# Two-layer mixer and expert kernel: weights in half blocks, expert row rings of five and six, and a reordered context prologue

## The reference, cut to what matters

```
mod = silu(c) @ ada_w[l] + ada_b[l]                  # 6 vectors of 1024: shift, scale, gate for mixer and experts
h = rmsnorm(x, norm_mix_g) * (1 + sc_m) + sh_m
proj = h @ w_in                                      # 1024 x 2048: q, k, v, hyena (3 x 256), gmlp (2 x 256)
mixed = concat(attention(q, k, v), hyena(...), chunk_gmlp(...)) @ w_out
x = x + g_m * mixed
h = rmsnorm(x, norm_ffn_g) * (1 + sc_f) + sh_f
s = (h @ peer_wq) . peer_keys                        # 8 heads x 2 halves x 128 keys
idx, gate = the best 16 of 16 x 16 pairs of keys, softmax over their scores     # per token and head
a = gelu(h . peer_u[idx]);  x = x + g_f * sum(gate * a * peer_v[idx])           # 128 experts per token
```

## Time and profile before

| | |
|---|---|
| median of 3 runs | 4637.51 us (4630.89 to 4637.74) |
| profiled execution, its own time | 4663.97 us |
| its span | 4662.2 us |
| TensorE / VectorE / ScalarE / GpSimd busy | 74% / 56% / 24% / 60% |
| moved by DMA | 1503.70 MB, mean 323 GB/s |
| mean granted TensorE clock | 0.876 |

### The profile page before, as it was taken

One profiled execution on the slowest core, in us unless ns is written; L12 is line 12 of the kernel. 1 busy time (PEld: TensorE's weight loads), 2 busy tenths in 40 slices (PEclk: granted clock), 3 DMA queues, 4 the chain that ended last, 5 costly groups with the idle time before them and its releaser, 6 DMA issues.

```text
span 4662.2 us, 37811 instructions
## 1 busy us (share of the span) xinstructions
PE 3442.7 (74%) x11256; PEld 1602.1 (34%) x11256; DVE 2632.0 (56%) x6503; ACT 1122.8 (24%) x2533; POOL 2806.0 (60%) x2564
## 2 busy tenths in 40 slices
PE   7869868766577767777776898786766676677777
PEld 3733434323123334332222444442322222222223
DVE  2166656456455565556666565564665666666661
ACT  3423223121212222212121432231211212121212
POOL 0035555566555666667777344565667777777774
PEclk8889888888788888889889899888878999998899
DMA  7468898789999999899999687887899999999997
GB/s 295 143 234 301 311 338 296 278 301 336 346 367 341 358 341 336 332 359 363 348 352 360 216 286 297 318 307 282 327 334 352 356 365 354 357 362 347 367 358 279
DMA packets 394680, 1503.70 MB, mean 323 GB/s; under 512 B 44396, under 2 KB 46126, under 8 KB 376432
## 3 DMA queue, kind: packets, MB, share of 16 engines
q0 software_dynamic: 368640, 1342.34, 78.9%
q1 hardware_dynamic: 25840, 158.96, 8.8%
HBM read 1498.24 MB, written 2.88 MB: 322 GB/s over the span
## 4 chain that ended last, share of the span: by engine, by line
POOL 30%; PE 24%; issue 18%; DMA 17%; DVE 7%; ACT 3%; SPq 0%; another core or an unknown queue 0%; DVEq 0%; POOLq 0%; ACTq 0%
POOL rows_ring L605 16%; POOL rows_ring L616 14%; DMA rows_ring<-in_peer_v,idx 7%; DMA rows_ring<-in_peer_v,turned_idx 7%; PE psum L928 6%; PE psum L920 5%; DVE rows_ring L1465 3%; PE psum L854 3%; PE psum L706 3%; DMA rows_ring<-in_peer_u,idx 2%; DMA ring<-in_ada 1%; PE psum L651 1%; PE psum L693 1%; PE psum L839 1%; PE psum L886 1%
## 5 line engine op out<-in xcount | busy, mean ns | idle before, releaser
L605 POOL DMA_INDIRECT rows_ring<-in_peer_u,idx x1280 | 1453.1, 1135 | 1198.5 <-DVE rows_ring L1465 587.3
L928 PE MATMUL psum<-rows_ring,diag 128*128 128x512 f32 x3072 | 1591.3, 667 | 634.0 <-DMA rows_ring<-in_peer_v,idx 581.4
L1465 DVE SCALAR_TENSOR_TENSOR rows_ring<-rows_ring,area 128x1024 f32<-128x1024 f32 x1280 | 1549.5, 1223 | 718.9 <-DMA rows_ring<-in_peer_u,idx 679.7
L928 PEld LDWEIGHTS psum<-rows_ring,diag 128*128 128x128 f32 x3072 | 618.4, 212 | 1567.2 <-issue 1453.3
L616 POOL DMA_INDIRECT rows_ring<-in_peer_v,idx x768 | 812.1, 1057 | 297.8 <-issue 211.3
L920 PE MATMUL psum<-rows_ring,diag 128*64 128x512 f32 x2048 | 641.1, 757 | 385.4 <-DMA rows_ring<-in_peer_v,turned_idx 376.8
L616 POOL DMA_INDIRECT rows_ring<-in_peer_v,turned_idx x512 | 540.5, 1056 | 334.2 <-PE psum L920 180.3
L1165 ACT ACTIVATE diag<-ident,turn 128x128 f32<-128x128 f32 x768 | 303.3, 401 | 1663.0 <-PE psum L928 1189.1
L920 PEld LDWEIGHTS psum<-rows_ring,diag 128*64 128x64 f32 x2048 | 160.4, 161 | 712.5 <-issue 661.5
L706 PE MATMUL psum<-area,ring 128*128 128x128 f32 (+1 forms) x832 | 240.9, 446 | 6.5 <-DMA ring<-in_win 6.5
L1474 DVE SCALAR_TENSOR_TENSOR turn<-acts,gate_s,gate_e 128x16 f32<-128x16 f32 x80 | 18.8, 235 | 382.3 <-ACT acts L1135 233.6
(11 more groups left out here) (185 smaller groups left out, 2864.3 us busy)
## 6 DMA issues: line engine op xcount, KB each, us to landing
ring<-in_ada SPq DMA_DIRECT2D x48, 1024.0 KB
ring<-in_win SPq DMA_DIRECT2D x32, 1024.0 KB
ring<-in_wout SPq DMA_DIRECT2D x24, 1024.0 KB
ring<-in_wq SPq DMA_DIRECT2D x24, 1024.0 KB
rows_ring<-in_peer_u,idx POOLq DMA_INDIRECT x1280
ring<-in_dft SPq DMA_DIRECT2D x12, 1024.0 KB
rows_ring<-in_peer_v,idx POOLq DMA_INDIRECT x768
rows_ring<-in_peer_v,turned_idx POOLq DMA_INDIRECT x512
```

The costliest lines, as they stand in the source:

```text
L605: pool.indirect_dma_start(row(0, k), None, peer_u, bass.IndirectOffsetOnAxis(ap=idx[v % IDX_PLACES][:, k:k + 1], axis=0)).then_inc(row_lan ...
L928: m = pe.matmul(acc[:, b, :], diag[:, (r + j) % 4, :], row(1, r + j)[:, b * 512:(b + 1) * 512], start=first and j == 0, stop=last and j == 1)
L1465: dve.scalar_tensor_tensor(out=row(0, k), in0=row(0, k), scalar=1.0, in1=h, op0=ALU.mult, op1=ALU.mult, accum_out=dots[:, k:k + 1]).then_i ...
```

## The change

`SLOTS` becomes 5, `HALF` is 1024 columns: weights come in half blocks (0.524 MB) into five places, 20 KB a partition instead of 32. `ROWS` becomes (5, 6): five rows for peer_u, six for peer_v. In `step_jobs` the `down` runs five places ahead and the `up` six (`spread` stays at four). `STREAM` is no longer written out: `blocks_of` names the half blocks that a job reads, and they are loaded in the order of first use in ORDER and freed after the last. The first 40 half blocks of layer 0's modulation go round the 11 places of the row rings, which no expert uses yet. SyncE still issues all loads in one order.

The context pass of layer 0 starts its mixer behind modulation block 3; blocks 4 to 9 stand among its jobs, 10 and 11 behind the first pick and the first gathers in the list (`_late`). The latent norm and filter of layer 0 move to the latent mixer, as in layer 1. `xT` is loaded in two parts: the context columns with four constants after eight half blocks, the latent ones with the rotary table and `swap` ahead of the first `wq` block (`latent_loads`). `dots` is doubled, so that `dot` waits for the gelu of two units before. VectorE walks `DVE_ORDER`, which gets the same jobs as `ORDER`; a function `behind` is added and not called.

```
-SLOTS = 4
-ROWS = 4
+HALF = BLOCK // 2
+SLOTS = 5
+ROWS = (5, 6)
@@ input_jobs
     if st == C_ and l == 0:
-        jobs = js("mod:0 mod:1 modT:0 mod:2 modT:1 mod:3 modT:2 mod:4 modT:3 rms:0 mod:5 modT:4 f1:0 mod:6 modT:5 f2:0 ")
-        jobs += latent("rms:0") + js("mod:7 modT:6 f3:4 mod:8 modT:7 hf:4") + latent("f1:0") + js("mod:9 modT:8")
-        jobs += latent("f2:0") + js("mod:10 modT:9 mod:11") + latent("f3:0 f3:1 f3:2 f3:3") + js("modT:10 modT:11")
...
+        jobs = js("mod:0 mod:1 modT:0 mod:2 modT:1 mod:3 modT:2 f1:0 modT:3 rms:0 f2:0 mod:4 f3:4 qk:0 modT:4 vt:4 hf:4 hs:0 "
+                  "hy:0 mod:5 ko:0 hy:1 modT:5 hy:2 hy:3 mod:6 hy:4 hy:5 modT:6 su:0 ut:0 su:1 mod:7 qk:1 sp:0 hs:1 modT:7 "
+                  "qk:2 hs:2 qk:3 mod:8 sp:1 hs:3 qk:4 modT:8 df:4 hs:4 mod:9 cv:0 cv:1 modT:9")
...
-        jobs = js("rms:0 f1:0 f2:0 f3:0 f3:1 f3:2 f3:3 hf:0 hf:1 hf:2 hf:3") if l else []
+        jobs = js("rms:0 f1:0 f2:0 f3:0 f3:1 f3:2 f3:3 hf:0 hf:1 hf:2 hf:3")
@@ step_jobs
-        unit("down", v + (k + ROWS) // TOPK, (k + ROWS) % TOPK)
+        unit("down", v + (k + ROWS[0]) // TOPK, (k + ROWS[0]) % TOPK)
-            pair("up", r + ROWS)
-            pair("spread", r + ROWS)
+            pair("up", r + ROWS[1])
+            pair("spread", r + 4)
@@
+_late = [("mod", 0, C_, 10), ("mod", 0, C_, 11), ("modT", 0, C_, 10), ("modT", 0, C_, 11)]
-ORDER, _taken = input_jobs(0, C_) + output_jobs(0, C_, 0) + _first, 0
+ORDER, _taken = input_jobs(0, C_) + output_jobs(0, C_, 0) + _first + _late, 0
+DVE_ORDER = list(ORDER)
@@
+def blocks_of(job):
+    kind, l, st, n = job
+    some = {"mod": ("ada", range(4 * n, 4 * n + 4)), "qk": ("win", [11 + n if n else 0]), "vt": ("win", range(1, 4)),
+            "hy": ("win", [4 + n]), "su": ("win", [10 + n]), "wo": ("wout", [n]), "wq": ("wq", [n])}
+    if st == L_:
+        some.update({"hf": ("dft", range(4)), "df": ("dftu", range(4)), "cv": ("dftu", range(4, 8))})
+    if kind in ("ka", "kb"):
+        some[kind] = ("keys", [1 if n > 1 else 0])
+    name, places = some.get(kind, ("", []))
+    return [(name, l, st, i) for i in places]
+
+LAST_USE = {}
+for _job in ORDER:
+    for _block in blocks_of(_job):
+        LAST_USE[_block] = (_job[0] + "_mm", done(*_job))
+STREAM = list(LAST_USE.items())
...
+    if _block[:2] == ("ada", 0) and _block[3] < 40:
+        _p, _n_rows = SLOTS + _n_rows % sum(ROWS), _n_rows + 1
+    else:
+        _p, _n_ring = _n_ring % SLOTS, _n_ring + 1
@@ SyncE
-                if n == SLOTS:
+                if n == 8:
                     small_loads(0)
                     const_loads()
-                if n >= SLOTS:
-                    name, value = STREAM[n - SLOTS][1]
+                if (kind, l, st, i) == ("wq", 0, C_, 0):
+                    latent_loads()
+                if FREED[n]:
+                    name, value = FREED[n]
                     sp.wait_ge(s[name], value)
@@ VectorE
-                if v and k == 0:
-                    dve.wait_ge(s["gelu_ready"], v)
+                if v > 1 and k == 0:
+                    dve.wait_ge(s["gelu_ready"], v - 1)
```

More of the change, by code:

```diff
@@ L210, in weave @@
 def weave(mixer, experts):
-    total, cost, taken, out = sum(ROOM[j[0]] for j in mixer), 0, 0, []
+    total, cost, taken, out = sum(ROOM[j[0]] for j in mixer) or 1, 0, 0, []
     for job in mixer:
@@ L219, in weave, with behind, stretch @@
     return out + experts[taken:]
-_first = [("pick", 0, 0, p) for p in range(PICK_PARTS)] + [("gexp", 0, 0, 0)] + [("down", 0, 0, k) for k in range(ROWS)]
+_first = [("pick", 0, 0, p) for p in range(PICK_PARTS)] + [("gexp", 0, 0, 0)] + [("down", 0, 0, k) for k in range(ROWS[0])]
 _steps = [_job for _v in range(len(UNIT) + 2) for _job in step_jobs(_v)]
-ORDER, _taken = input_jobs(0, C_) + output_jobs(0, C_, 0) + _first, 0
[L227 to L231, removed]
+_late = [("mod", 0, C_, 10), ("mod", 0, C_, 11), ("modT", 0, C_, 10), ("modT", 0, C_, 11)]
+ORDER, _taken = input_jobs(0, C_) + output_jobs(0, C_, 0) + _first + _late, 0
+DVE_ORDER = list(ORDER)
+def behind(jobs, n):
+    out, held, dots = [], [], 0
+    for job in jobs:
+        if job[0] in ("dot", "pick", "down", "up"):
+            while held and held[0][0] <= dots:
+                out.append(held.pop(0)[1])
+            dots += job[0] == "dot"
+            out.append(job)
+        else:
+            held.append((dots + n, job))
+    return out + [job for _, job in held]
+def stretch(mixer, upto, also=0):
+    global ORDER, DVE_ORDER, _taken
+    end = _steps.index(upto) + also
+    jobs = weave(mixer, _steps[_taken:end])
+    ORDER += jobs
+    DVE_ORDER += jobs
     _taken = end
@@ L280 @@
 TURNED_BEFORE = {j: TURNED[i - 1] for i, j in enumerate(TURNED) if i}
[L283 to L307, removed]
-            for _i in range(2, 4):
-                _b("dftu", _i, "cv_mm", "cv", 1)
-        for _part, (_t, _end) in enumerate(PARTS[_st]):
-            for _i in range(4 * _part, 4 * _part + 4):
-                _b("wout", _i, "wo_mm", "wo", 2 * _i + 1)
-            for _i in range(4 * _part, 4 * _part + 4):
-                _b("wq", _i, "wq_mm", "wq", 2 * _i + 1)
-            _b("keys", _part, "kb_mm", "kb", 2 * _end - 1)
@@ L486, in mixer_peer_kernel @@
         y_stored = [sem("y_stored0"), sem("y_stored1")]
-        landed = [sem(f"landed{k}") for k in range(SLOTS)]
-        row_landed = [[sem(f"{name}_landed{k}") for k in range(ROWS)] for name in ("down", "up")]
+        landed = [sem(f"landed{k}") for k in range(PLACES)]
+        row_landed = [[sem(f"{name}_landed{k}") for k in range(n)] for name, n in zip(("down", "up"), ROWS)]
         def qk_dst(st, n):
@@ L1505, in _ @@
             dve.tensor_tensor(stacked[:], ident[:, 0:64], ident[:, 64:128], ALU.add).then_inc(s["stacked_ready"], 1)
-            for job in ORDER:
+            for job in DVE_ORDER:
                 kind, a, b, n = job
```

158 lines of the change are left out of this document (88 added, 70 removed).

## The result

The changed kernel takes 4278.47 us (median of 4 runs, 4274.45 to 4289.31) against 4637.62 us for the kernel before, a ratio of 0.922 with a 95% interval of 0.9181 to 0.9259. I had forecast 4557 us. The direction was right and the size was not: 359 us less instead of 80.

A forecast was written before the change was run, and what follows sets the result against it. It took the expert-row gathers, holding 78.9% of the DMA engines' span, as the bound. Its terms, -62 + 35 - 70 + 12 + 5 = -80 us, took 4637.5 to 4557 us; range 4465 to 4635, the sum's own 4515 to 4600.

The forecast's parts named there:

- Part 1: Prologue: reordered loads and context mixer bring the first gather to 189 us, 62 us earlier, bounds 45 to 75.
- Part 2: First stage behind the first gather: moved latent and modulation work costs 35 us, between 5 and 48.
- Part 3: Row rings of 5 and 6: 70 us gained, about 10 in expert stretches; bounds nothing to half of 421.
- the cap of 421 us: All stages behind the prologue: the DMA's idle time, (1 - share) x length, limits what longer row rings can gain.
- the average wait of 2.9 us: GpSimd at the first ring: 587.3 / 200, the period of one row, so one row more can swallow a typical wait.
- Part 4: Weights in half blocks, five places: costs 12 us, between 0 and 210, plus 5 us for smaller packets.
- Part 5: VectorE's order list, unused `behind` and doubled dots: no instruction moves, 0 us.
- B: Row rings buy a third of the idle DMA, 140 us: 4487 us; chance 0.17.
- A: Row rings buy nothing, as TensorE and the DMA set the woven stages: 4617 us; chance 0.19.
- C: Slower: half blocks of weights come late behind the first gather, up to 4753 us at 1 us lateness; chance 0.14.
- Rival D: Moved latent work costs all it saved, 48 with only 45 won at the front: 4587 us; chance 0.50.
- the signs that I had named: Row-ring waits clearly below 850 us, woven stages' DMA share up 0.03 or so, expert stretches' rates hardly moving.

The follow-up runs named there:

- e11: Kernel after with the latent norm and filter of layer 0 back in the context pass, in one piece behind its convolution: 4284.88 us, ratio 0.9213.
- e1: Kernel after with both row rings back at four rows, the rest of the change kept: 4662.39 us, ratio 1.0018 to the kernel before.
- e6: Kernel after with row rings of four and four and eight half-block places for the weights instead of five: 4633.52 us, ratio 0.9949.
- e7: Kernel after with second-table gathers of 512 columns instead of 1024, a quarter less DMA traffic, sums wrong: 4329.90 us, ratio 0.9307.
- e15: Kernel after with VectorE's dots in two halves and second-table gathers of 512 columns, sums wrong: 4121.72 us, ratio 0.8849.
- e3: Kernel after with four rows for the first table and six for the second: 4376.48 us, ratio 0.9399.
- e2: Kernel after with five rows for the first table and four for the second: 4653.91 us, ratio 1.0004.
- e10: Kernel after with rings of four and four and the second table's gathers two places ahead of the add instead of four: 5504.72 us, ratio 1.1821.
- e13: Kernel after with five rows for each table: 4603.31 us, ratio 0.987.
- e16: Kernel after with each VectorE dot in four pieces of 256 columns: 4215.87 us, ratio 0.9051.

## Why the prediction was wrong, by its own steps

**Part 1 was right in its time, by errors that cancel.** The first gather came at 191.7 us for 189. The key projection began at 55.84, 8 us later than I had it: the norm's first square came at 41.30 for 34 and the norm took 11.4 us for 10.2, while the second sine and the filter product cost no more than I had. The chain from there to the end of the convolution took 62 us for 65, and the latent tokens cost nothing at the first query block. e11 shows what the 59 us hang on: with the latent norm and filter back in front, in one piece, nothing of them remains. So they are mostly work moved behind the first gather. What the new order would bring with these jobs spread among others, as they stood before, was not tried.

**Part 2 was about right, with a reservation.** The stage became 470 us for 475 forecast. With the old rings, however, units 0 to 8 take 530 us for 470 (e1), 519 with eight weight places (e6), so the moved work costs 49 to 60 us there and I had 35; the longer rings gave 36 back. With the old rings and eight weight places the whole reordered prologue brings 0.5% (e6), 24 us for my 27.

**Part 3 is the step that failed: 384 us for 70** (e1 against the kernel after; 371 by the ratios). That is also beyond the 210 us that I had named as the upper bound. Three readings in it were wrong.

First, the cap of 421 us from (1 - DMA share) x length. The share counts time in which packets are under way, not what could be moved: the same share of 0.97 to 1.01 held 357, 387 and 399 GB/s, and a quarter fewer bytes changed no expert unit (e7, e15). So I held the expert stretches for full and gave them 10 us; they gave 94 + 35 = 129 us. By their own sum they were GpSimd's: 32 x (1.11 + 0.30) = 45.1 us and about 1.8 us of waits make the 47.0 of before, and 32 x (1.053 + 0.30) = 43.3 make the 43.6 of after. So about half of what a unit gained is waits and half is shorter issues. Why they became shorter stays open. Between the 57th and the 80th list 104 issues took over 1.3 us, for 151 before; but e3, where GpSimd hardly waits for a dot there (0.7 us in 1100), has 179, an issue mean of 1.125 us and therefore a unit of 45.8.

Second, the rings' waits taken by name. 587 us against 263 made the first ring look like the one to lengthen, and its one new row the one that counts. It is worth nothing alone (e2). Much of the wait for VectorE came from the second table's ring, passed on through one common order of jobs: it fell by 204 us in e3 and rose by 975 in e10 with the first ring unchanged. Whether the late row itself (theory B of e10) or the gathers held up behind it (theory D of e10) weighs more is not shown.

Third, the average wait of 2.9 us set against one row's period. An add takes two rows, so one pair is the step in which the second ring works (e13). I tried to get the size from the round trip of a pair. The issues of the kernel after from 3144 to 4210, with the median us to landing behind the comma:

```profile
rows_ring<-in_peer_u,idx POOLq DMA_INDIRECT x391, 6.4
rows_ring<-in_peer_v,idx POOLq DMA_INDIRECT x364, 6.4
```

A pair costs two issues of 1.35 us, that landing, an add of some 2 us, and up to two gathers of the first table queued ahead: some 14 us, an estimate from these rows. Set against the average time that two pairs bridge it does not explain the gain. In the expert stretch before they bridge 2 x 47 / 8 = 11.8 us, less than 14, and yet GpSimd waited there only 23 of 1160 us for the second ring. In units 8 to 16 they bridge 2 x 479 / 64 = 15 us, more than 14, and there the two rows brought 59 us. What is shown is where they help, beside mixer jobs (239 of 268 us in e3). That a mixer job ahead of an add uses up a margin so small, and the third pair covers it, is argued and not shown.

**Part 4 was under-sized:** the five places cost 29 us (e6 against e1) for 12. The 5 us for smaller packets were not tried by themselves; the hardware queue moved its 158.97 MB in 10.1% of 4272 us, 368 GB/s for 387 before, near the 365 that I had as the worst. **Part 5** was not tried by itself.

**Rivals.** B had the sign and named the second table's side, and 140 us of 384. A would have left as they were; C was the right fear for 29 us. Rival D, which I gave the largest chance, holds with the old rings: e1's first list comes 60 us earlier and its units 0 to 8 take 60 us longer. It says nothing of the rings, and they made the result. None had the second ring's pairs as what counts, and my range of 4465 to 4635 rested on a cap that was none. Of the signs that I had named, the waits for the row rings fell as forecast (850 to 559 us), but the DMA share of three woven stages rose by 0.07 to 0.10 for 0.03, and the rates of the expert stretches, which should hardly move, rose by 24 and 30 GB/s. The page of the Trainium skill that I weighed (DMA: Bandwidth & Descriptors, Specifications: about 358 GB/s from HBM for a core) would have stopped the expert stretches at 357. The page gets that figure by dividing the bandwidth of two cores by two, and here one core runs. They ran at 387 and 399 GB/s; the measurement decides.

## What to carry to other kernels

Give a ring its rows in the unit in which the consumer takes them, and try each ring by itself before trusting either a wait's size or an average round trip; transfers that look full by busy share are proved to be the limit only by taking bytes away. Where engines share one order of jobs, a wait's name is its last link: move the suspected cause later and see which wait grows. And add up the queue that issues (issue time plus gap, times count) before believing that the transfers behind it are the limit.

## What the runs showed of the hardware that I had not expected

A gather's issue on GpSimd that starts while VectorE runs a `scalar_tensor_tensor` on float32 in SBUF with an accumulator can be held until that instruction ends, and then ends 0.8 us later (98 of 98 issues over 1.3 us; 0.939 us is the mean when no dot runs). Halving the VectorE instruction is worth 102 us in 4278, although it adds 103 us of VectorE work; with quarters (e16) no issue between the 57th and the 80th list takes over 1.3 us. The Trainium skill (SBUF — State Buffer, Who interferes with whom) tells of a lock of this kind for VectorE's two-port modes, in which whoever issues first has the shared ports for its whole instruction and the other is blocked. It also has an instruction with two SBUF inputs, as the dot is, contend with a GpSimd instruction that reads SBUF, as a gather does for its indices, and infers that the writing of descriptors is not touched by that. The held issues of this case agree with a lock of one kind or the other; no run here tells which.

Less data can cost time: with half rows in the second table the issues grew from 1.05 to 1.15 us, and the kernel was 0.9% slower by the two ratios. They did not meet more dots (349 of 686 issues began beside one, 386 of 737 in the kernel after), but those that did took 1.356 us for 1.156, and 192 instead of 98 took over 1.3. Why stays open.
